# Streaming the moving operand of every product from its last column to its first

## The reference

```python
for layer in range(DEPTH):
    h = rms_norm(x, mix_norm[layer])
    x = x + hybrid_mixer(h, w_in[layer], ...)          # 1024 x 3584 projection, causal convolution,
                                                       # causal pooling, gates, 1024 x 1024 output
    h = rms_norm(x, ffn_norm[layer])
    if layer % 2 == 0:
        x = x + swiglu(h, dense_w_gate[i], dense_w_up[i], dense_w_down[i])   # d_ff 2816
    else:
        x = x + moe_ffn(h, router_w[i], moe_w_gate[i], moe_w_up[i], moe_w_down[i])  # top 2 of 8, d_ff 3584
return rms_norm(x, final_norm)
```

## Time and profile before

| what | value |
|---|---|
| median of three runs | 1425.84 us |
| the profiled execution | 1425.18 us |
| its span, first to last instruction | 1423.6 us |
| TensorE matmul busy | 1409.4 us, 99% |
| TensorE weight load busy | 1168.6 us, 82% |
| VectorE busy | 1174.7 us, 83% |
| ScalarE busy | 986.9 us, 69% |
| DMA | 445.96 MB, 313 GB/s on average |

### The profile page before, as it was taken

The page is one execution under the profiler, slowest core; times in us unless marked ns, Lnnn a source line. Parts: engine busy times, 40 slices in busy tenths (PEclk is TensorE's granted clock), DMA queues, the critical chain, the costliest instruction groups (busy, mean ns, idle before and its releaser), DMA issues.

```text
span 1423.6 us, 18360 instructions
## 1 busy us (share of the span) xinstructions
PE 1409.4 (99%) x6506; PEld 1168.6 (82%) x6506; DVE 1174.7 (83%) x1068; ACT 986.9 (69%) x876; POOL 207.9 (15%) x249
## 2 busy tenths in 40 slices
PE   9999999999999999999999999999999999999997
PEld 7888888888888888888888888888888888888885
DVE  6987544548987998889899898888989989888896
ACT  7765444347765877867877777786787777778674
POOL 6840000005831001001001001000100100100010
PEclk9999999999999999999999999999999999999999
DMA  9656555545548899999999999999999999999990
GB/s 359 222 169 215 178 181 198 183 162 196 175 164 310 283 386 378 371 370 409 375 382 372 390 367 371 388 370 369 412 372 384 370 391 366 371 389 373 366 411 33
DMA packets 197552, 445.96 MB, mean 313 GB/s; under 512 B 8400, under 2 KB 19968, under 8 KB 197504
## 3 DMA queue, kind: packets, MB, share of 16 engines
q1 hardware_dynamic: 192496, 432.57, 80.4%
q0 software_dynamic: 2304, 8.39, 2.2%
q10 hardware_dynamic: 2704, 4.38, 0.9%
HBM read 437.97 MB, written 7.34 MB: 313 GB/s over the span
## 4 chain that ended last, share of the span: by engine, by line
issue 58%; PE 34%; POOL 4%; DVE 2%; ACT 1%; DMA 0%; POOLq 0%; ACTq 0%; DVEq 0%
PE bank L1467 10%; PE bank L1469 10%; PE bank L1468 10%; POOL small L611 2%; POOL gates L614 2%; DVE w_lo L989 1%; POOL sums L621 1%; PE bank L1528 1%; DVE bank L1038 1%; PE bank L1631 0%; PE bank L1593 0%; ACT w_hi L654 0%; PE bank L1763 0%; PE bank L1587 0%; DVE tokA L1104 0%
## 5 line engine op out<-in xcount | busy, mean ns | idle before, releaser
L989 DVE TENSOR_TENSOR w_lo<-raw,w_hi 128x2048 fp32r<-128x2048 f32 x256 | 582.9, 2292 | 134.8 <-ACT w_hi L654 134.6
L654 ACT ACTIVATE w_hi<-raw 128x2048 fp32r<-128x2048 f32 x256 | 488.6, 1913 | 200.2 <-PE bank L1469 199.8
L1467 PE MATMUL bank<-w_hi,dT_hi 128*128 128x512 f32 (+1 forms) x756 | 296.4, 392 | 0.0
L1469 PE MATMUL bank<-w_hi,dT_lo 128*128 128x512 f32 (+1 forms) x756 | 293.2, 388 | 0.0
L1468 PE MATMUL bank<-w_lo,dT_hi 128*128 128x512 f32 (+1 forms) x756 | 292.6, 387 | 0.0
L1467 PE MATMUL bank<-w_hi,cT_hi 128*128 128x512 f32 x492 | 194.3, 395 | 0.0
L1469 PE MATMUL bank<-w_hi,cT_lo 128*128 128x512 f32 x492 | 191.7, 390 | 0.0
L1468 PE MATMUL bank<-w_lo,cT_hi 128*128 128x512 f32 x492 | 191.6, 390 | 0.0
L1469 PEld LDWEIGHTS bank<-w_hi,dT_lo 128*128 128x128 f32 x756 | 142.0, 188 | 29.4
L1467 PE MATMUL bank<-w_hi,hT_hi 128*128 128x512 f32 x416 | 164.4, 395 | 1.1 <-DVE w_lo L1086 1.0
L1468 PEld LDWEIGHTS bank<-w_lo,dT_hi 128*128 128x128 f32 x756 | 142.2, 188 | 28.1
(11 more groups left out here) (256 smaller groups left out, 1865.8 us busy)
## 6 DMA issues: line engine op xcount, KB each, us to landing
raw<-in_moe_w_gate_dram SPq DMA_DIRECT2D x96, 1024.0 KB, 7.5
raw<-in_moe_w_up_dram SPq DMA_DIRECT2D x72, 1024.0 KB, 10.3
raw<-in_moe_w_down_dram SPq DMA_DIRECT2D x72, 1024.0 KB, 8.9
raw<-in_w_in_dram SPq DMA_DIRECT2D x20, 1024.0 KB, 7.1
mix<-in_moe_w_up_dram SPq DMA_DIRECT2D x16, 1024.0 KB, 8.8
gates<-in_moe_w_down_dram SPq DMA_DIRECT2D x16, 1024.0 KB, 11.3
gates<-in_moe_w_up_dram SPq DMA_DIRECT2D x16, 1024.0 KB, 8.8
work<-in_moe_w_down_dram SPq DMA_DIRECT2D x16, 1024.0 KB, 11.5
```

Of the source, the lines that this page charges most:

```text
L654: act.activation(w_hi[split_place(u, seen.item is not None)][:, 0:width], place[slot][:, 0:width], ACT.Copy).then_inc(hi_ready, 1)
L989: dve.tensor_tensor(w_lo[split][:, 0:width], place[slot][:, 0:width], w_hi[split][:, 0:width].bitcast(F32), ALU.subtract).then_inc(lo_read ...
L1467: nc.tensor.matmul(dst, a_hi, b_hi, start=start, stop=False)
L1469: return nc.tensor.matmul(dst, a_lo, b_hi, start=False, stop=stop)
```

## The change

One line is added to `product`. It turns the last dimension of three access patterns around: the destination and the two moving operands. The moving column that was read last is read first, and its result is written to the last column of the bank, so that each result lands where it did before. The stationary operands, the order of the matmuls, the flags that begin and end a sum, the semaphores and all other matmuls stay.

```diff
@@ -1464,6 +1464,7 @@
 
             def product(dst, a_hi, a_lo, b_hi, b_lo, start, stop):
 
+                dst, b_hi, b_lo = dst[:, ::-1], b_hi[:, ::-1], b_lo[:, ::-1]
                 nc.tensor.matmul(dst, a_hi, b_hi, start=start, stop=False)
                 nc.tensor.matmul(dst, a_hi, b_lo, start=False, stop=False)
                 return nc.tensor.matmul(dst, a_lo, b_hi, start=False, stop=stop)
```

## The result

The changed kernel takes 1460.14 us (median of four runs, 1458.58 to 1461.41) beside 1425.93 us for the kernel before (median of four, 1425.17 to 1429.56). The ratio is 1.0233, with a 95% interval of 1.0219 to 1.0247: it is slower by 34.2 us. The forecast was no change.

A forecast was written before the change was run, and what follows sets the result against it. The prediction took TensorE to bound the kernel from the first products to the last. Its terms, 0 + 0 + 0 + 0 + 0, left the time at 1425.8 us against the median, with a full range of 1420 to 2680 us.

The forecast's parts named there:

- The bound: Whole kernel: TensorE bounds it from first product to last, busy 1409.4 of 1423.6 us, with 5808 matmuls of 512 columns touched.
- Instructions: In `product`: none removed or added, each of the three matmuls stays one matmul; cost 0.
- weight loads: Stationary loads on TensorE: 188 ns of the 226.7 ns beside the matmul ahead, operand not turned; cost 0.
- waits, queues: Semaphores and SyncE's DMA queue: no wait added or moved, no new step ahead of the queue; cost 0.
- the distance between sums: Successive matmuls into one bank: a column is written again one matmul later, as before, 226.7 ns; cost 0.
- The stream itself: Moving read and bank write with step minus one: the unknown, taken as 0 because the same pairs and fours are visited.
- rival C: Each touched matmul: fixed part grows by about 8 ns, 49 us more, so 1474 us; chance 0.04.
- Rival A: Moving read or bank write: descending stream halves its rate, 0.84 ns a column, so 2612 or 2675 us; chance 0.24.
- B: Product stream: slower by another factor, 1738 us if a column costs a quarter more, or about 5160 us; chance 0.08.
- D: Each touched matmul: fixed part shrinks by at most 12.5 ns, so 1353 us, perhaps 1400 us; chance 0.06.
- E: Program build: the change doesn't reach the hardware, time again 1425.8 us; chance 0.03, within the forecast's 0.58.
- the likeliest case: Whole kernel: all terms 0, no change, 1425.8 us against the median, own range 1423 to 1429 us; chance 0.58.

The follow-up runs named there:

- f_write_reversed: Model's kernel with ScalarE and VectorE storing moving blocks reversed, TensorE reading forward and only writing the bank reversed: 1426.12 us beside 1426.09 before.
- m2: TensorE alone, 52 streams of 48 matmuls varying stationary columns, start columns, run lengths and steps: reversed with 32 stationary columns 233.3 ns, plain forward 226.6 to 226.9.
- m3: TensorE alone, 72 streams of 32 matmuls at varied moving and stationary start columns: with 512 columns, forward 226.6 to 236.6 ns, reversed 233.1 to 235.6.
- m4: TensorE alone, 37 streams, among them both operands moved together: by 8, 16 or 32 columns 227.5 to 228.1 ns, by 4 231, by 1 238.
- f_run2: The change with pairs kept (runs of 2 ascending columns, last run first, read and write) in the model's kernel: 1462.03 us beside 1425.55 before.
- m1: TensorE alone, streams of 48 matmuls varying direction of read and write, length, run length and type: forward 226.7 ns, read reversed 233.3, write reversed 227.1.
- f_early16: Model's kernel, nothing reversed, 16-column spare tensor allocated behind w_lo so raw, w_hi and w_lo lie 64 bytes earlier: 1457.11 us beside 1426.04 before.

## Why the prediction was wrong

**The bound** was right. TensorE is the bound in all of the run: the mean product took 6.1 ns more, 5808 of them make 35.4 us, and the time grew by 34.2; DMA, VectorE and ScalarE only followed. (The 1.0 us that the working calls one of TensorE's longest waits is the total of two, the longest 0.7. Nothing hangs on it.)

**Instructions, weight loads, waits, queues, the distance between sums**: right, 0 each. The weight load's record is 188 ns before and after in the largest groups, the counts are equal, and f_write_reversed shows that the order in which a bank is written is free.

**The stream itself** is the step that failed. The working took 0 on the ground that a descending read visits the same words in the same pairs and fours. The runs showed 6.7 ns for each 512-column matmul, all of it in the read. The reason given was about the moving operand alone. m2, m3 and m4 show that the pace of a 512-column stream depends on two reads: where the moving and the stationary operand lie relative to each other, and whether the moving one ascends for at least 64 columns at a time (runs of 32 took 232.8 ns). In the kernel before, the tensors allocated between the two operands are all multiples of 64 columns long, and 226.7 ns is the favoured pace; the reversal leaves it for the ordinary one.

**The bounds** of that step, from -12.5 ns to +203 ns, held the value but were of no help. The row that had the size was in the working: 235 ns in four distances after the 256-column products. It was read there as "the fixed part can move by 8 ns" and given 0.04 as rival C, with 1474 us. It was the same form from the same tiles that had 226.7 ns from 99.12 us on: a direct sight of what a forward stream costs off its fast pace. Priced by it, rival C was the nearest of all (49 us for 34.2). The guess that the surplus would be alike in both lengths was wrong as well: the 256-column form became 1.3 ns faster.

**Rival A** (half rate, 0.24) and **B** fall, in mechanism too (f_run2). **D**: nothing went below 226.6 ns. **E** falls: the time changed, and the order reached the chip.

**The range**, 1420 to 2680 us, held the time only because it reached to rival A; the likeliest case's own range, 1423 to 1429, did not. With the chance on 0.58 for no change, the case "a stream has more than one pace with the same bytes" was missing as a rival of some weight.

**What stays open.** Why a relative distance of 64 columns matters with 512 columns and not with 448, and why a descending read never reaches the fast pace, isn't shown. That the two reads of SBUF meet in some part of the memory fits the common shift in m4; that fewer stationary columns didn't help speaks against a simple count of meetings. A stream without loads of the stationary operand wasn't tried. How the surplus depends on the length isn't explained either. It is 0 at 320 and 336 columns, 1.7 ns at 288, 2.5 to 4.0 at 352, 384, 416, 448 and 480, and 6.7 at 512 (m1, m2 and m3, start column 0), and some of these forward streams, as the one with 448, may not have been at their own fast pace.

## What to carry to other kernels

A float32r matmul stream that bounds a kernel has a fast and an ordinary pace, 226.7 and 233.3 ns for 512 columns. With 512 columns and 128 stationary ones, keep moving and stationary tiles on starts that differ by a multiple of 256 bytes (and lie on 32-byte multiples); for another length measure the starts anew, since with 448 columns a start of column 64 was slow. In the same way, read the moving operand upwards in runs of 64 columns or more, and put any reversal into the write to the bank or into the ScalarE or VectorE pass that makes the operand, where it was free. When the trace of before shows one and the same instruction form at two distances, 227 and 235 ns here, take the other one as a price to be reckoned with, before reasoning from geometry.

## What the hardware showed that was not expected

- The start column of either operand is worth as much as the direction in a 512-column stream: 226.7 against 233 ns, and up to 236.6 at an odd column (m3_placement); 31 us in the model from 64 bytes (f_early16).
- bfloat16 streams take 216 ns forward, reversed or from an odd column, and plain float32 ones 215.9 ns for 256 columns both ways; of the three types only float32r showed a cost of direction.
- VectorE with its output and one of its sources reversed takes 2298 ns a unit, 2300 before; ScalarE with its output reversed 1920 in both (f_write_reversed).
- A float32r stream that was interrupted starts at the ordinary pace and reaches the fast one after five to ten matmuls (the trace of before).
